# Hybrid streaming layer: x transposed by the host and multiplied strip by strip, two tiles at once, with other stages moved

## The chip, the cores and the metric

One core of a Trainium2 chip runs the whole program; the other cores are idle. The metric is the device time of one execution in microseconds. A core has five engines with a queue each: TensorE (PE, matrix products), VectorE (DVE), ScalarE (ACT), GpSimd (POOL) and SyncE (SP), which issues nearly all DMAs. They run side by side and meet through semaphores. The order of the instructions of each engine is written out by hand in this kernel.

## The reference

One layer for 1024 prompt frames and 32 sample frames together (T = 1056 columns), all in float32:

```python
n = rmsnorm(h, g_mix[l])
z = n @ w_in[l]                       # (1056 x 1024) @ (1024 x 3072)
a_out, s_re, s_im = ssm_branch(u_ssm, ...)      # S5: 32 groups, 64 complex states each
p_out, p_hist = pool_branch(u_pool, ...)        # trailing means of 2, 4, 8, 16 frames
merged = sigmoid(gate_ssm) * a_out + sigmoid(gate_pool) * p_out
h = h + merged @ w_out[l]
n2 = rmsnorm(h, g_ffn[l])
h = h + (silu(n2 @ w_ffn_gate[l]) * (n2 @ w_ffn_up[l])) @ w_ffn_down[l]   # inner width 2816
y = rmsnorm(h, g_final)
```

The factor 1/rms of rmsnorm is a number for each frame, so it commutes with the product: the kernel multiplies x times gain by the weights first and scales the columns of the result behind it. The outputs are y, the last complex states and the last 15 inputs of the pooling branch, for both groups.

## The kernel before

**Precision and slabs.** Each product runs in three passes on split operands: w_hi by x_hi, w_hi by x_lo, w_lo by x_hi. A slab is 128 columns of a weight matrix, 128 x 1024. SyncE loads it into one of two `stage` slots, ScalarE's `split` (line 705) copies it to w_hi, GpSimd's `lo` (line 891) makes w_lo. A tile is 128 output rows by 1056 columns: eight k steps, three passes and three column blocks of 352 give 72 matmuls (`tile`, line 461) into `bank_a` or `bank_b`. It waits until the tile two before has been taken out of its bank (`evac_done`). Slab s may be loaded when `lo_ready` has reached s - 1.

**Head.** SyncE loads x in nine tiles of 128 frames. TensorE turns each one (line 486), VectorE writes it twice, as xg (times g_mix) and as x_raw (line 964), the second for a spill to `xt_scratch`, from which hT is read much later. ScalarE squares the rows (line 721) and makes x_hi, GpSimd makes x_lo. Fifteen small loads bring the parameters, which TensorE turns also (`turn_parameters`). Tile 0 goes by passes (line 514), tiles 1 to 3 follow; these four are the state-space input u. `inverse_root` makes 1/rms on VectorE with a root on ScalarE, `rstd_rows` (line 473) spreads it over all partitions by products of ones with `diag`, `take_rows` copies it to `rstd_row`, and `take_u` (on line 934, where nearly all two-operand operations of VectorE are) scales u into UT.

**State-space parameters.** VectorE computes in a long row of small operations an angle, whose sine ScalarE takes (line 739), then BD, BB, PW, and from these CA (ends at line 1121) and WT. TensorE multiplies BD by CA to K (line 534), turns WT to W (line 545, copied by ScalarE at line 749). GpSimd clears TO when WT is done, then SyncE puts K_sb into TO with sixteen loads (line 348) and fetches U from `u_scratch` with eight (line 354). 128 small products of W and U (line 582) give V, copied into S (line 768). Then VectorE scans S along time in steps spread over the pool groups.

**Pool groups.** Group g is five tiles: the pooled input, two gates and two short tiles of nine matmuls on the pooled values pl_hi and pl_lo. VectorE sums and scales; `gate_t` (line 1277) is scaled by the second product. Both short tiles use bank_b, so the second waits for the scaling of the first. After group 0 stands the V stage. SyncE's order around it: slab 6, u_scratch, slab 7 (pool weights), TO, U, then slabs 8 and 9 for group 1, and CA_st.

**The rest.** Gates, the products of TO with U and CA_st with S_st (lines 603, 604), four transposes of the last states (line 609), the gated units, the output product, the feed-forward part and the final norm. It is not changed but for where hT comes from.

## Time and profile before

| | |
|---|---|
| median of three runs | 1383.84 us (1382.25 to 1385.69) |
| span of the profiled execution | 1384.4 us |
| TensorE, VectorE | busy 1334.2 us, 681.9 us |
| ScalarE, GpSimd | busy 304.8 us, 307.8 us |
| moved by DMA | 95.64 MB, mean 69 GB/s |

All times of the trace are from the start of the span of the profiled execution. Read a line of a timeline as: start, duration, engine, line of the kernel, operation, what it writes and reads; several equal ones in a row are one line with their count, and the bracket tells how long the engine was idle before and what released it. Matmuls overlap, so the duration of one is longer than the distance between two.

### The profile page before, as it was taken

Reading aid. Unit: us, or ns where it says so; the run is one execution under the profiler, and the core shown is the slowest. Engines: PE = TensorE matmul, PEld = TensorE weight load, DVE = VectorE, ACT = ScalarE, POOL = GpSimd, SP = SyncE. Lnnn points to the kernel's source line nnn. Section 1 sums busy time; section 2 is a strip of 40 time slices with the busy share of each in tenths; the row PEclk is TensorE's granted clock in tenths of the full one; section 3 lists DMA queues with packets and bytes.
Section 4 is the critical chain, followed back from the end, with each engine's and each line's share of the span. In section 5 each row is a group of like instructions: output and inputs, shape, how many; then the busy total and the mean of one; then the engine's idle time right before and its main releaser. Section 6 shows DMA issues by size and latency. Waiting matters only on the chain.

```text
span 1384.4 us, 19221 instructions
## 1 busy us (share of the span) xinstructions
PE 1334.2 (96%) x8306; PEld 1320.3 (95%) x8306; DVE 681.9 (49%) x696; ACT 304.8 (22%) x325; POOL 307.8 (22%) x131
## 2 busy tenths in 40 slices
PE   6999699999999999999999999999999999999997
PEld 5988599999999999999999999999999999999996
DVE  5895279860546643324434343434343434343355
ACT  6112221142432222212111111111111111111124
POOL 6111121221222224412222222222222222211210
PEclk9999899999999999999999999999999999999998
DMA  8408641224303351111111111111111111111103
GB/s 258 112 16 145 96 113 66 80 74 101 131 25 92 107 182 40 44 43 46 47 45 45 45 45 45 45 45 43 42 40 42 44 45 45 45 45 46 46 16 126
DMA packets 134895, 95.64 MB, mean 69 GB/s; under 512 B 15165, under 2 KB 122973, under 8 KB 134858
## 3 DMA queue, kind: packets, MB, share of 16 engines
q1 hardware_dynamic: 134794, 95.10, 24.5%
q8 instruction: 26, 0.43, 0.1%
q14 instruction: 11, 0.09, 0.0%
q10 hardware_dynamic: 64, 0.02, 0.0%
HBM read 74.40 MB, written 17.43 MB: 66 GB/s over the span
## 4 chain that ended last, share of the span: by engine, by line
PE 81%; DVE 11%; issue 3%; SPq 2%; DMA 2%; POOL 0%; ACT 0%; DVEq 0%
PE bank_a L461 39%; PE bank_b L461 38%; DMA stage<-in_w_in 1%; DVE f_u L934 1%; DVE hT L934 1%; SPq L348 1%; PE aux L582 1%; DVE tmp_a L934 1%; DVE tmp_b L934 1%; SPq L354 1%; DVE sc_a L934 1%; SPq L322 1%; DVE S L934 1%; DVE pt L934 0%; DVE UT L934 0%
## 5 line engine op out<-in xcount | busy, mean ns | idle before, releaser
L891 POOL TENSOR_TENSOR w_lo<-stage,w_hi 128x1024 fp32r<-128x1024 f32 x110 | 260.8, 2371 | 996.3 <-ACT w_hi L705 996.3
L705 ACT ACTIVATE w_hi<-stage 128x1024 fp32r<-128x1024 f32 x110 | 114.0, 1037 | 797.4 <-PE bank_b L461 495.4
L461 PE MATMUL bank_b<-hg_hi,w_hi 128*128 128x352 f32 x528 | 114.8, 326 | 0.0
L461 PE MATMUL bank_b<-hg_lo,w_hi 128*128 128x352 f32 x528 | 114.7, 325 | 0.0
L461 PE MATMUL bank_a<-hg_lo,w_hi 128*128 128x352 f32 x528 | 114.2, 324 | 0.0
L461 PE MATMUL bank_a<-hg_hi,w_hi 128*128 128x352 f32 x528 | 113.8, 323 | 0.0
L461 PE MATMUL bank_b<-hg_hi,w_lo 128*128 128x352 f32 x528 | 113.8, 324 | 0.0
L461 PE MATMUL bank_a<-hg_hi,w_lo 128*128 128x352 f32 x528 | 113.2, 323 | 0.0
L934 DVE TENSOR_TENSOR hT<-bank_a,hT 128x1056 f32<-128x1056 f32 x48 | 60.2, 1255 | 80.6 <-PE bank_a L461 80.6
L934 DVE TENSOR_TENSOR hT<-bank_b,hT 128x1056 f32<-128x1056 f32 x48 | 60.4, 1258 | 76.2 <-PE bank_b L461 76.2
L934 DVE TENSOR_TENSOR f_u<-bank_b,rstd_row 128x1056 f32<-128x1056 f32 x22 | 27.7, 1257 | 142.6 <-PE bank_b L461 142.6
L461 PEld LDWEIGHTS bank_b<-hg_hi,w_lo 128*128 128x128 f32 x528 | 90.6, 189 | 0.0
L461 PEld LDWEIGHTS bank_b<-hg_hi,w_hi 128*128 128x128 f32 x528 | 90.3, 189 | 0.1
L461 PEld LDWEIGHTS bank_b<-hg_lo,w_hi 128*128 128x128 f32 x528 | 90.3, 188 | 0.0
L461 PEld LDWEIGHTS bank_a<-hg_hi,w_lo 128*128 128x128 f32 x528 | 90.1, 188 | 0.0
L461 PEld LDWEIGHTS bank_a<-hg_lo,w_hi 128*128 128x128 f32 x528 | 89.8, 188 | 0.0
L461 PEld LDWEIGHTS bank_a<-hg_hi,w_hi 128*128 128x128 f32 x528 | 89.8, 188 | 0.0
L461 PE MATMUL bank_a<-x_hi,w_hi 128*128 128x352 f32 x408 | 88.5, 325 | 0.8 <-ACT S L768 0.8
L461 PE MATMUL bank_a<-x_lo,w_hi 128*128 128x352 f32 x408 | 88.2, 324 | 0.0
L461 PE MATMUL bank_a<-x_hi,w_lo 128*128 128x352 f32 x408 | 87.6, 323 | 0.0
L934 DVE TENSOR_TENSOR f_g<-bank_a,rstd_row 128x1056 f32<-128x1056 f32 x22 | 27.7, 1257 | 112.6 <-PE bank_a L461 112.6
L461 PE MATMUL bank_b<-x_hi,w_hi 128*128 128x352 f32 x336 | 72.7, 324 | 0.7 <-ACT W L749 0.7
(262 smaller groups left out, 2355.8 us busy)
## 6 DMA issues: line engine op xcount, KB each, us to landing
stage<-in_w_in SPq DMA_DIRECT2D x24, 512.0 KB, 3.7
stage<-in_w_ffn_gate SPq DMA_DIRECT2D x22, 512.0 KB, 3.7
stage<-in_w_ffn_up SPq DMA_DIRECT2D x22, 512.0 KB, 3.6
stage<-in_w_ffn_down SPq DMA_DIRECT2D x22, 512.0 KB, 3.7
mp_scratch<-gate_t SPq DMA_DIRECT2D x8, 528.0 KB, 3.5
pool_t<-mp_scratch SPq DMA_DIRECT2D x8, 528.0 KB, 3.8
hT<-xt_scratch SPq DMA_DIRECT2D x8, 528.0 KB, 7.5
x_t<-in_x_prompt SPq DMA_DIRECT2D x8, 512.0 KB, 7.0
```

The source lines that it names most:

```text
L322: sp.dma_start(dst, src).then_inc(prm_in, 16)
L348: sp.dma_start(TO[16 * i:16 * i + 16, g2:G:2, 16 * j:P], K_sb[16 * g2:16 * g2 + 16, :, 0:P - 16 * j]).then_inc(to_in, 16)
L354: sp.dma_start(U[16 * i:16 * i + 16, :, :], u_dram[:, L - 1 - i, :].rearrange("(g h) c -> h g c", h=H)).then_inc(u_in, 16)
L461: mm = pe.matmul(banks[:, b, 0:BLK], w[:, slot, col:col + P], x[:, k, b * BLK:(b + 1) * BLK], start=(i == 0 and step == 0), stop=(i == len ...
L582: mm = pe.matmul(aux[64 * g2:64 * g2 + 64, (pr + 1) % 2, comp * NCG:(comp + 1) * NCG], W[:, comp, pr, 64 * g2:64 * g2 + 64], U[:, 2 * pr + ...
L705: act.activation(w_hi[:, slot, 0:cols], stage[:, slot, 0:cols], ACT.Copy).then_inc(hi_ready, 1)
L891: pool.tensor_tensor(w_lo[:, slot, 0:cols], stage[:, slot, 0:cols], w_hi[:, slot, 0:cols], ALU.subtract).then_inc(lo_ready, 1)
L934: return dve.tensor_tensor(out, a, b, op)
```

## The change

- The host passes x transposed and the parameters laid out as the kernel wants them; two outputs leave in a layout that the host puts back.
- TensorE's transposes of x and of parameters, x_raw, xg and the spill go. SyncE loads eight strips of 128 channels by 1056 frames. ScalarE makes x_hi from each with the gain as its scale, VectorE x_lo. TensorE multiplies each strip into tiles 0 and 1 as it comes; the w_lo pass of both follows.
- The rows of x are still loaded and squared, now beside the tiles and through four buffers. The row products stand behind tile 2.
- ScalarE copies u unscaled out of the banks (`raw_u`); VectorE scales the four tiles in SBUF (`scale_u`) once the rows are there, behind PW.
- VectorE takes up pool group 0 (`take_pool`) between CA and WT; TensorE makes K behind tile 5 and W behind tile 6. ScalarE splits slab 8 ahead of taking W, with the root, the sine and the sigmoids in other places.
- SyncE fetches U ahead of TO.
- The short tiles of a pool group use both banks, which change roles from group to group; the loop over groups 1 to 3 on TensorE is unrolled. The pool history leaves by ScalarE's queue from UP, the last states by one copy and one store.

```diff
-            for tt in range(6):
+                if tt >= XT_SLOTS:
+                    sp.wait_ge(x_squared, tt - XT_SLOTS + 1)
+                sp.dma_start(x_t[0:tok(tt), tt % XT_SLOTS, :], src).then_inc(x_in[tt], 16)
+            sp.dma_start(gains[:], t_in["p_gains"]).then_inc(gains_in, 16)
+            load_xs(0)
+            slab(0, 0, [(slab3(0)[:, 0:4], w_in[:, 0:4, 0:P])])
+            slab(1, 1, [(slab3(1)[:, 0:4], w_in[:, 0:4, P:2 * P])])
+            load_xs(1)
+            load_xs(2)
+            for s in range(2):
+                sp.dma_start(slab3(s)[:, 4:8], w_in[:, 4:8, s * P:(s + 1) * P]).then_inc(second_in[s], 16)
+            for k in range(3, KD):
+                load_xs(k)
+            sp.dma_start(prm[:], t_in["p_prm"]).then_inc(prm_in, 16)
+            sp.dma_start(ident[:], t_in["c_ident"]).then_inc(consts_in, 16)
+            for tt in range(XT_SLOTS):
                 load_x(tt)
-            slab(0, 0, [(slab3(0), w_in[:, :, 0:P])])
...
-            spill_x(sp, 0)
-            slab(1, 1, [(slab3(1), w_in[:, :, P:2 * P])])
...
-            sp.dma_start(inv_count[:], t_in["c_inv_count"]).then_inc(inv_in, 16)
-            with nc.allow_non_contiguous_dma(reason="512 skip weights, one per (channel, group)"):
-                for dst, src in prm_loads:
-                    sp.dma_start(dst, src).then_inc(prm_in, 16)
-            for tt in range(4, TT):
-                spill_x(sp, tt)
             for s in (2, 3):
                 slab(s, s % 2, [(slab3(s % 2), w_in[:, :, s * P:(s + 1) * P])])
+            sp.dma_start(b_raw[:], t_in["p_b"]).then_inc(bc_in, 16)
+            sp.dma_start(CT[:], t_in["p_c"]).then_inc(bc_in, 16)
+            sp.dma_start(inv_count[:], t_in["c_inv_count"]).then_inc(inv_in, 16)
+            sp.dma_start(pool_hist[:], t_in["p_hist"]).then_inc(inv_in, 16)
+            sp.dma_start(state0[:], t_in["p_state"]).then_inc(inv_in, 16)
+            sp.dma_start(d_skip[:], t_in["p_skip"]).then_inc(inv_in, 16)
+            for tt in range(XT_SLOTS, TT):
+                load_x(tt)
             slab(4, 0, [(slab3(0), w_in[:, :, W_SSM:W_SSM + P])])
             slab(5, 1, [(slab3(1), w_in[:, :, 2 * W_SSM + D:2 * W_SSM + D + P])])
...
-            sp.wait_ge(evac_done, KS)
+            sp.wait_ge(u_scaled, KS)
             sp.dma_start(u_dram.rearrange("(n p) j c -> p n j c", p=P), UT[:, :, :, :]).then_inc(ut_out, 16)
             pool_w_slab(0)
+            sp.wait_ge(ut_out, 16)
+            for i in range(L):
+                sp.dma_start(U[16 * i:16 * i + 16, :, :],
+                             u_dram[:, L - 1 - i, :].rearrange("(g h) c -> h g c", h=H)).then_inc(u_in, 16)
             sp.wait_ge(k_ready, 1)
             sp.wait_ge(to_zero, 1)
...
+            for k in range(KD):
+                pe.wait_ge(x_hi_ready, k + 1)
+                for n in range(2):
+                    if k == 0:
+                        pe.wait_ge(first_half, n + 1)
+                    if k == KD // 2:
+                        pe.wait_ge(hi_ready, n + 1)
+                    pair_pass(k, n, w_hi, x_hi, k == 0, False)
+                pe.wait_ge(x_lo_ready, k + 1)
+                for n in range(2):
+                    pair_pass(k, n, w_hi, x_lo, False, False)
+            for n in range(2):
+                pe.wait_ge(lo_ready, n + 1)
                 for k in range(KD):
...
+                    mm = pair_pass(k, n, w_lo, x_hi, False, k == KD - 1)
+                mm.then_inc(tile_done, 1)
+            pe.wait_ge(lo_ready, 3)
+            tile(2, bank_a, 0, ALL, x_hi, x_lo)
+            rstd_rows(1, diag)
+            pe.wait_ge(lo_ready, 4)
+            tile(3, bank_b, 1, ALL, x_hi, x_lo)
+            def turn_k():
+                pe.wait_ge(ca_ready, 1)
...
-            def pool_group(g, after_first=None):
+            def pool_group(g):
                 s0, t0 = 4 * g + S_POOL, 5 * g + T_POOL
+                odd, even = (bank_b, bank_a) if g % 2 else (bank_a, bank_b)
                 pe.wait_ge(lo_ready, s0 + 1)
-                tile(t0, bank_a, 0, ALL, x_hi, x_lo)
-                if after_first is not None:
-                    after_first()
+                if g == 0:
+                    pe.wait_ge(row_used, 1)
+                tile(t0, odd, 0, ALL, x_hi, x_lo)
                 pe.wait_ge(lo_ready, s0 + 2)
-                tile(t0 + 1, bank_b, 1, ALL, x_hi, x_lo)
+                tile(t0 + 1, even, 1, ALL, x_hi, x_lo)
+                if g == 0:
+                    turn_k()
                 pe.wait_ge(lo_ready, s0 + 3)
-                tile(t0 + 2, bank_a, 0, ALL, x_hi, x_lo)
+                tile(t0 + 2, odd, 0, ALL, x_hi, x_lo)
+                if g == 0:
+                    turn_w()
                 pe.wait_ge(lo_ready, s0 + 4)
                 pe.wait_ge(pooled_lo, g + 1)
                 hi, lo = pl_hi[:, :].unsqueeze(1), pl_lo[:, :].unsqueeze(1)
-                tile(t0 + 3, bank_b, 1, [(0, 0)], hi, lo)
-                if not isinstance(g, int):
-                    pe.wait_ge(np_evac, g)
-                pe.transpose(aux[0:HIST, 0, 0:P], UP[:, SEQ:SEQ + HIST], ident[:, :])
-                pe.transpose(aux[0:HIST, 0, P:2 * P], UP[:, T + HIST:T + 2 * HIST], ident[:, :]).then_inc(np_turned, 1)
-                pe.wait_ge(evac_done, t0 + 4)
-                tile(t0 + 4, bank_b, 1, [(P, 0)], hi, lo)
-            pool_group(0, turn_w)
+                tile(t0 + 3, even, 1, [(0, 0)], hi, lo)
+                tile(t0 + 4, odd, 1, [(P, 0)], hi, lo)
+            pool_group(0)
...
+            def half(s, h):
+                act.wait_ge((second_in if h else stage_in)[s], 16)
+                cols = slice(h * SLAB // 2, (h + 1) * SLAB // 2)
+                act.activation(w_hi[:, s, cols], stage[:, s, cols], ACT.Copy).then_inc(hi_ready if h else first_half, 1)
+            def take_hi(k):
+                act.wait_ge(xs_in[k], 16)
+                act.activation(x_hi[:, k, :], xs[:, k, :], ACT.Copy, scale=gains[:, 0, k:k + 1]).then_inc(x_hi_ready, 1)
+            def square(tt):
+                act.wait_ge(x_in[tt], 16)
+                row = x_t[0:tok(tt), tt % XT_SLOTS, :]
+                act.activation(row, row, ACT.Square, accum_out=ss[0:tok(tt), 0, tt:tt + 1]).then_inc(x_squared, 1)
+            def raw_u(n):
+                act.wait_ge(tile_done, n + 1)
+                banks = bank_b if n % 2 else bank_a
+                for b0, nb, c0, nch, to in ((0, 2, 0, 44, 0), (2, 1, 88, 40, 88), (2, 1, 128, 4, NCP + 1)):
+                    o = UT[:, n, :, to:to + nb * nch].rearrange("p j (b c) -> p b c j", b=nb)
+                    off = 0 if c0 != 128 else 40 * L
+                    i0 = banks[:, b0:b0 + nb, off:off + nch * L].rearrange("p b (c j) -> p b c j", j=L)
+                    ins = act.activation(o, i0, ACT.Copy)
+                ins.then_inc(evac_done, 1)
+            act.wait_ge(gains_in, 16)
+            take_hi(0)
+            half(0, 0)
+            half(1, 0)
+            take_hi(1)
+            take_hi(2)
+            half(0, 1)
+            half(1, 1)
+            for k in range(3, KD):
+                take_hi(k)
...
+            square(0)
+            square(1)
+            split(2, 0, landed(2), 1)
+            raw_u(0)
+            square(2)
+            split(3, 1, landed(3), 2)
+            raw_u(1)
+            for tt in range(3, TT):
+                square(tt)
...
             root(1)
+            split(4, 0, landed(4), 3)
+            act.wait_ge(row_ready, 1)
+            raw_u(2)
             act.wait_ge(angle_ready, 1)
             act.activation(pt[:, 8:10, :], pt[:, 6:8, :], ACT.Sin).then_inc(sine_ready, 1)
-            for s in range(2, 6):
-                split(s, s % 2, landed(s), s - 1)
-            act.wait_ge(x_lo_ready, TT)
+            split(5, 1, landed(5), 4)
+            raw_u(3)
+            split(6, 0, landed(6), 5)
             for q in range(4):
                 act.wait_ge(k_turn, q + 1)
...
             for g in range(4):
                 s0, t0 = 4 * g + S_POOL, 5 * g + T_POOL
-                split(s0 + 2, 0, landed(s0 + 2), t0 + 1)
+                if g:
+                    split(s0 + 2, 0, landed(s0 + 2), t0 + 1)
                 act.wait_ge(pooled_ready, g + 1)
                 act.activation(pl_hi[:, :], (sum_b if g % 2 == 0 else sum_a)[:, 0:T], ACT.Copy).then_inc(pooled_hi, 1)
-                for r in range(2):
-                    split(s0 + 3 + r, 1 - r, landed(s0 + 3 + r), t0 + 2 + r, cols=(2 * P, SLAB)[r])
-                    act.wait_ge(evac_done, t0 + 2 + r)
-                    act.activation(gate_t[:, r, :], gate_t[:, r, :], ACT.Sigmoid).then_inc(gp_sig, 1)
+                act.dma_start(t_out["pool"][:, 0, g, :], UP[:, SEQ:SEQ + HIST]).then_inc(pool_out, 16)
+                act.dma_start(t_out["pool"][:, 1, g, :], UP[:, T + HIST:T + 2 * HIST]).then_inc(pool_out, 16)
+                split(s0 + 3, 1, landed(s0 + 3), t0 + 2, cols=2 * P)
+                if g == 0:
+                    split(s0 + 4, 0, landed(s0 + 4), t0 + 3)
+                    take_w()
+                    sigmoid_p(0, 0)
+                    sigmoid_p(0, 1)
+                else:
+                    sigmoid_p(g, 0)
+                    split(s0 + 4, 0, landed(s0 + 4), t0 + 3)
+                    sigmoid_p(g, 1)
                 split(s0 + 5, 1, landed(s0 + 5), t0 + 5)
...
-            for s in range(1, 5):
+            for s in range(7):
                 lo(s, s % 2)
             pool.wait_ge(wt_ready, 1)
             pool.memset(TO[:, :, :], 0.0).then_inc(to_zero, 1)
-            for s in range(5, S_GATE):
+            for s in range(7, S_GATE):
                 lo(s, s % 2, 2 * P if s % 4 == 3 else SLAB)
...
+            dve.wait_ge(gains_in, 16)
+            for k in range(KD):
+                dve.wait_ge(xs_in[k], 16)
+                dve.wait_ge(x_hi_ready, k + 1)
+                dve.scalar_tensor_tensor(x_lo[:, k, :], xs[:, k, :], gains[:, 0, k:k + 1], x_hi[:, k, :], MUL,
+                                         SUB).then_inc(x_lo_ready, 1)
...
+            def scale_u(n):
+                dve.wait_ge(evac_done, n + 1)
+                tt_(UT[:, n, :, :], UT[:, n, :, :], rstd_u[:, :, :], MUL).then_inc(u_scaled, 1)
...
-            take_rows(1)
-            take_u(0)
+            dve.wait_ge(x_squared, TT)
+            dve.wait_ge(consts_in, 16)
+            inverse_root(1, ss[:, 0, :], diag)
             dve.wait_ge(sine_ready, 1)
...
-            take_u(1)
+            take_rows(1)
+            dve.tensor_copy(rstd_u[:, :, 0:NCP], rstd_row[:, 0:SEQ].rearrange("p (c j) -> p j c", j=L))
+            dve.memset(rstd_u[:, :, NCP:NCP + 1], 0.0)
+            dve.memset(UT[:, :, :, NCP:NCP + 1], 0.0)
+            then(dve.tensor_copy(rstd_u[:, :, NCP + 1:NCG], rstd_row[:, SEQ:T].rearrange("p (c j) -> p j c", j=L)))
+            for n in range(KS):
+                scale_u(n)
+            dve.wait_ge(u_scaled, KS)
...
-            take_u(2)
+            take_pool(0)
             dve.wait_ge(ca_ready, 1)
...
-                for r, banks in enumerate((B3, A3)):
+                for r in range(2):
                     dve.wait_ge(tile_done, t0 + 2 + r)
                     if g:
                         dve.wait_ge(mp_out[r], 16 * g)
-                    tt_(b3(gate_t[:, r, :]), banks, b3(rstd_row[:, :]), MUL).then_inc(evac_done, 1)
+                    elif r == 0:
+                        dve.wait_ge(to_in, 32 * L)
+                    tt_(b3(gate_t[:, r, :]), bank3(t0 + 1 + r), b3(rstd_row[:, :]), MUL).then_inc(evac_done, 1)
```

## Rows read from the trace of the kernel before

**Rows 1.** The page, busy us, share and number of instructions of each engine.

```profile
PE 1334.2 (96%) x8306; PEld 1320.3 (95%) x8306; DVE 681.9 (49%) x696; ACT 304.8 (22%) x325; POOL 307.8 (22%) x131
```

**Rows 2.** Waits of TensorE in the whole span: us in total, times, longest.

```profile
PE bank_b L461 <- DVE gate_t L1277: 8.0, 4, 2.9
PE aux L582 <- DMA U<-u_scratch: 6.7, 1, 6.7
PE bank_a L486 <- DMA x_t<-in_x_prompt: 4.8, 1, 4.8
```

**Rows 3.** Windows: busy us and count per engine, PEclk, DMA share, GB/s.

```profile
10.00:15.00 5.00, 4.40 (x20) 3.66 (x19) 5.00 (x6) 5.00 (x8) 4.50 (x2) 1.00 1.03 370
...
26.00:30.00 4.00, 3.96 (x14) 3.99 (x15) 0.00 (x0) 2.17 (x2) 4.00 (x3) 0.50 0.80 148
...
205.00:280.00 75.00, 73.65 (x458) 73.31 (x457) 65.11 (x123) 12.44 (x15) 14.64 (x7) 1.00 0.21 71
```

**Rows 4.** Timeline of the head: start, us, engine, line, operation, count, idle before.

```profile
10.32 1.04 ACT L721 ACTIVATE x_sq<-x_t 128x1024 f32<-128x1024 f32 x1
...
26.05 6.55 PE L514 MATMUL bank_a<-x_hi,w_hi 128*128 128x352 f32 x24 [2.39 <-DVE x_raw L964]
...
35.99 1.36 DVE L934 TENSOR_TENSOR diag<-ident,ss 128x1152 f32<-128x1152 f32 x1
...
45.42 1.95 PE L473 MATMUL aux<-diag,ones 128*128 128x128 f32 x16
...
47.63 0.75 PE L461 MATMUL bank_b<-x_hi,w_hi 128*128 128x352 f32 x3
```

**Rows 5.** Timeline of VectorE, 48 to 180 us.

```profile
52.53 0.91 DVE L1062 MEMSET BD<- 128x1024 f32 x1
...
66.36 2.13 DVE L934 TENSOR_TENSOR UT<-bank_b,rstd_row 128x704 f32<-128x704 f32 x3
...
73.39 4.63 DVE L934 TENSOR_TENSOR CA<-tmp_a,tmp_b 128x2304 f32<-128x2304 f32 x1
...
87.50 2.27 DVE L934 TENSOR_TENSOR tmp_a<-BB,PW 128x2048 f32<-128x2048 f32 x1
```

**Rows 6.** Timeline of GpSimd, 37 to 180 us.

```profile
72.39 3.23 POOL L891 TENSOR_TENSOR w_lo<-stage,w_hi 128x1024 fp32r<-128x1024 f32 x1 [9.23 <-ACT w_hi L705]
101.21 3.52 POOL L904 MEMSET TO<- 128x4096 f32 x1 [25.60 <-DVE WT L934]
```

**Rows 7.** Timeline of TensorE, 80 to 180 us.

```profile
85.74 8.84 PE L534 MATMUL aux<-CA,BD 128*32 128x128 f32 x64 [2.96 <-DVE CA L1121]
...
164.11 0.74 PE L461 MATMUL bank_a<-x_hi,w_hi 128*128 128x352 f32 x3 [0.78 <-ACT S L768]
```

**Rows 8.** Timeline of SyncE's DMA queue, 37 to 180 us.

```profile
107.56 12.36 SPq L348 DMA_DIRECT2D TO<-K_sb  x16
```

**Rows 9.** The chain that ended last, 0 to 420 us: start, us, what.

```profile
133.97 15.51 DMA stage<-in_w_in
...
152.79 10.56 PE aux L582 x120
...
284.02 3.00 PE bank_b L461 x9
...
326.19 0.61 PE aux L609 x4
```

**Rows 10.** Timeline of ScalarE, 37 to 180 us.

```profile
94.61 0.59 ACT L745 ACTIVATE K_sb<-aux 32x512 f32<-32x512 f32 x1 [1.16 <-PE aux L534]
...
108.19 1.09 ACT L749 ACTIVATE W<-aux 128x512 f32<-128x512 f32 x2 [0.26 <-PE aux L545]
...
124.47 1.28 ACT L759 ACT_TABLE_LOAD   x1
125.76 1.09 ACT L759 ACTIVATE gate_t<-gate_t 128x1056 f32<-128x1056 f32 x1
```

**Rows 11.** The page, DMA issues: count, KB each, median us from issue to landing.

```profile
stage<-in_w_in SPq DMA_DIRECT2D x24, 512.0 KB, 3.7
```

More of the change, by code:

```diff
@@ L136, in hybrid_layer @@
         ut_at = q_space + G * P + 2 * PAIRS * 9 * H + 2 * PAIRS * P
-        _, diag = overlay(("pad4", [P, ut_at], F32), ("diag", [P, TT, P], F32))
+        w_at = q_space + G * P + 2 * PAIRS * 9 * H
+        _, x_t = overlay(("pad17", [P, w_at], F32), ("x_t", [P, XT_SLOTS, D], F32))
+        _, diag, rstd_u = overlay(("pad4", [P, w_at], F32), ("diag", [P, TT, P], F32), ("rstd_u", [P, L, NCG], F32))
         _, UP, sum_a, sum_b = overlay(("pad5", [P, ut_at], F32), ("UP", [P, T + 2 * HIST], F32),
@@ L507, in _ @@
-            pe.wait_ge(xraw_ready, TT)
-            for w, x, ready, count in ((w_hi, x_hi, x_hi_ready, TT), (w_lo, x_hi, lo_ready, 1), (w_hi, x_lo, x_lo_ready, TT)):
-                pe.wait_ge(ready, count)
-                if w is w_hi:
-                    pe.wait_ge(hi_ready, 1)
-                for k in range(KD):
-                    for b in range(3):
-                        mm = pe.matmul(bank_a[:, b, 0:BLK], w[:, 0, k * P:(k + 1) * P], x[:, k, b * BLK:(b + 1) * BLK],
-                                       start=(w is w_hi and x is x_hi and k == 0), stop=(x is x_lo and k == KD - 1))
-                if w is w_hi and x is x_hi:
-                    turn_parameters()
@@ L518, in _, with pair_pass @@
-            mm.then_inc(tile_done, 1)
-            for s in range(4):
-                if s:
-                    pe.wait_ge(lo_ready, s + 1)
-                    tile(s, bank_b if s % 2 else bank_a, s % 2, ALL, x_hi, x_lo)
-                if s == 0:
-                    pe.wait_ge(prm_used, 2)
-                    rstd_rows(1, diag)
-            pe.wait_ge(ca_ready, 1)
-            pe.wait_ge(row_used, 1)
-            for q in range(4):
-                if q >= 2:
-                    pe.wait_ge(k_evac, q - 1)
-                for i in range(4):
-                    for comp in range(2):
-                        mm = pe.matmul(aux[0:2 * H, q % 2, i * P:(i + 1) * P], BD[:, comp, 4 * q + i, :],
-                                       CA[:, comp, 4 * q + i, 0:P], start=(comp == 0), stop=(comp == 1))
-                mm.then_inc(k_turn, 1)
+            def pair_pass(k, n, w, x, first, last):
+                banks = bank_b if n else bank_a
+                for b in range(3):
+                    mm = pe.matmul(banks[:, b, 0:BLK], w[:, n, k * P:(k + 1) * P], x[:, k, b * BLK:(b + 1) * BLK],
+                                   start=first, stop=last)
+                return mm
@@ L585, in _ @@
             pe.wait_ge(v_evac, PAIRS)
-            with pe.Fori(1, 4) as g:
+            for g in range(1, 4):
                 pool_group(g)
@@ L1085, in bc_h @@
                 return ap.unsqueeze(2).to_broadcast([P, PAIRS, H])
[L1086 to L1087 removed]
+            dve.wait_ge(bc_in, 32)
             t1, t2 = [t[:, 0:PAIRS * H].rearrange("p (q h) -> p q h", h=H) for t in (tmp_a, tmp_b)]
@@ L1138, in _ @@
             tt_(wt[1], mid_of(tmp_a), mid_of(tmp_b), ADD).then_inc(wt_ready, 1)
-            then(dve.memset(UT[:, :, :, NCP:NCP + 1], 0.0))
-            take_u(3)
             dve.wait_ge(k_evac, 4)
+            dve.wait_ge(inv_in, 64)
             lag0 = K_sb[:, :, 0:H]
@@ L1431 @@
     r = run_bass_kernel_spmd(nc, [{f"in_{n}": a for n, a in arrays.items()}], core_ids=[0])
-    return tuple(r.results[0][f"out_{n}"] for n in OUTPUTS)
+    y_p, y_s, state, pool = (r.results[0][f"out_{n}"] for n in OUTPUTS)
+    state = state.reshape(2, NS, 2, 2, PAIRS).transpose(2, 3, 4, 0, 1).reshape(2, 2, 1, 1, G, NS)
+    pool = pool.transpose(1, 3, 2, 0).reshape(2, 1, 1, HIST, W_POOL)
+    return (y_p, y_s, state[0, 0], state[0, 1], pool[0], state[1, 0], state[1, 1], pool[1])
```

311 lines of the change are left out of this document (96 added, 215 removed).

## The prediction

> **What bounds the kernel now.** I read the page first: TensorE is busy for 96% of the span [rows 1]. Each idle stretch of TensorE is therefore time, and almost nothing else is. Its waits [rows 2] add up to little. But a busy TensorE is not always a useful one: until 26 us it only turns x. The first product comes at 26.05 us, its 24 matmuls take 6.55 us, and tile 1 begins only at 47.63 [rows 4], although the DMA engines bring 370 GB/s in the meantime [rows 3]. From there on a tile of 72 matmuls takes 11.6 us. So the head holds about 25 us that a better order could give back. Then I read VectorE from 50 to 113 us: it has no gap. It makes PW, CA and WT one after the other [rows 5]. Behind WT hang the clearing of TO on GpSimd [rows 6], sixteen loads of TO [rows 8], the loads of U and then one weight slab that needs 15.5 us [rows 9]; TensorE waits 3.0 us for CA [rows 7] and 6.7 for U [rows 2]. The question is thus not what the head saves but whether this second chain starts earlier.
>
> I call T the moment at which the first tile of pool group 1 starts (line 461, behind the 128 small products of line 582). Before, T is 164.1 us [rows 7].
>
> **The change, part by part.**
>
> *Head.* The 72 transposes of x, the copies to x_raw and the spills go. The first strip of x is 528 KB behind one small load, like the first x_t behind the identity: it lands at 4.8 us [rows 2]. A table load of 1.28, a scaled copy of 1056 elements 1.1, half a slab 0.6 [rows 10]: TensorE starts at 7.8. Everything up to strip 7 is 5.4 MB, at 370 GB/s [rows 3] in by 16.6 us, and TensorE reaches strip 7 at about 24: the transfers are hidden. Two tiles are 23.3 us, and a cold start costs 6.55 - 3.9 = 2.6 us (granted clock 0.50, the 1.2 GHz level, in 26 to 30) [rows 3, 4]. GpSimd makes w_lo of both slabs while VectorE makes x_lo from two SBUF operands. In the trace such an operation stands still while GpSimd's runs: CA's third takes 4.63 us, not 2.6 (2.27 for 2048 elements), beside w_lo at 72.39, which is itself stretched [rows 5, 6]. Bounds here are 0 and 2.2 us, as TensorE has some reserve; I take 0.8. Tile 1 ends at 7.8 + 23.3 + 2.6 + 0.8 = 34.5 us, against 47.6 + 11.6 = 59.2 before: 25 us.
>
> *From tile 1 to the sine.* ScalarE now does, in its written order, the split of slab 3 (1.06), the raw copy of u (not in the trace: 1056 elements from PSUM, between 1.1 for a contiguous copy [rows 10] and 2.13 for VectorE's strided UT [rows 5]; I take 1.8, nearer the same access), and squares 3 to 8. Loads 6 to 8 wait for squares because of the four buffers, and are there some us before their turn. Six squares at 1.04 + 0.19 are 7.4 us [rows 4]. Then table and root 1.5, VectorE's five small steps and diag 2.4 [rows 4]. The split of slab 4 comes right behind the root, so GpSimd's w_lo meets diag: 2.2 us more by [rows 5, 6], none if they miss each other; I take 2.2. Then row products on TensorE 2.3 [rows 4], raw copy of tile 2 1.8, table and sine 1.5. Sum: 34.5 + 1.06 + 1.8 + 7.4 + 1.5 + 2.4 + 2.2 + 2.3 + 1.8 + 1.5 = 56.5 us. BD and PW come behind it; before, BD began at 52.5 [rows 5]. So the 25 us are gone here: queued squares and row sums stand before the sine. TensorE waits some 5 us for diag.
>
> *From the sine to CA.* BD, BB and PW take 52.53 to 66.3 = 13.8 us with one meeting with GpSimd [rows 5]: 70.3. Taking the rows 1.4 (71.7): only now may tile 4 start, while tile 3 ended near 65. Then rstd_u and its fills 2.0 and four scalings (1.26 contiguous to 2.13 strided [rows 5]; both operands are contiguous, so 1.26) 5.1; they replace four take_u of 2.13. CA takes 68.4 to 85.7 = 17.3 [rows 5, 7]: ready at 96.1. TensorE from 71.7 with two tiles and 2.0 for a cold start (below the 2.6 seen) is at 97.0. It sets the start of the K products, not 85.7 as before.
>
> *From K to WT.* The last K copy ends 9.5 us behind the first product (85.7 to 95.2 [rows 7, 10]) and stands ahead of pl_hi in ScalarE's order; pl_hi and pl_lo take 2.4. VectorE, which now pools group 0 ahead of WT, waits for both: 97.0 + 9.5 + 2.4 = 108.9. WT takes 87.5 to 101.2 = 13.7 us [rows 5, 6]: 122.6.
>
> *From WT to T.* Clearing TO 3.5 [rows 6]; sixteen issues 12.4 [rows 8]; then slab 8, which ScalarE must split before it may take W. U is fetched ahead of TO here, so slab 8 no longer stands behind U and lands 3.7 us after its issue, the median [rows 11]; the other bound is 15.5 [rows 9]. 122.6 + 3.5 + 12.4 + 3.7 = 142.2. The split 1.06, four pairs of W copies at 1.35 = 5.4, two short tiles 3.5 (two sigmoids and a table load beside them, 3.5), split of slab 9 1.06, the 128 small products 10.6 [rows 9] and 0.7 around them. T = 164.5. Against 164.1 it is 0.4 us later: what the wait for U cost before is back as a wait for W behind slab 8.
>
> *Behind T.* The second half of each pool product goes to the other bank now and no longer waits for the scaling of the first: 8.0 us in four groups [rows 2]. The one in group 0 is inside T. In group 1 I count 1.3 us (the gate on VectorE still has to come), in group 2 1.2; in group 3 VectorE is 2.5 us ahead by then, and the half that took 3.0 us on a low clock [rows 9] instead of 1.7 is shorter: 2.3. The four state transposes (0.6 [rows 9]) and the wait ahead of them save 1.0. Sum 5.8. The smaller moves (one state store, laid out parameters, hT read from the input) lie beside products of TensorE that run without a gap after 330 us: nothing. The seven parameter loads ahead of slab 4 cost SyncE some 0.4 us each in a stretch where that slab isn't due for 5 us; their landing is covered likewise.
>
> *Sum.* 1384.4 + 0.4 - 5.8 = 1379.0 in the profiled execution. That one is 0.56 us over the median of the runs, so 1378.4 us.
>
> **Rivals.**
> 1. The head's gain survives. It would need CA by about 85; then tiles 4 and 5 run without pause: 1384.4 - 22 - 2 is about 1360. For it speak the 25 us; against it the written order: sine behind six squares, root and rows. Chance 0.12.
> 2. VectorE holds the pool groups. It is 87% busy from 205 to 280 [rows 3]; if its scan steps set the pace, only 2 of the 5.8 us are kept: 1382. Chance 0.20.
> 3. Slower: slab 8 lands late. If it needs 15.5 us also behind TO's transfers, ScalarE can't take W and T moves by 11.8: 1390. It decides from a landing of 9 us on (13 for clearly slower). For it: this very wait stood at 133.97 [rows 9]; against it: there it stood behind U. Chance 0.12.
> 4. The head doesn't do what it says: the clock stays low through most of two tiles, or strided copies on ScalarE take 2.5 us: 1384. Chance 0.08.
> 5. A table switch costs more than its load. If ScalarE stood for as long again behind the loads for root and sine, both come 2.6 us later: 1381. In the trace a sigmoid follows its load at once (124.47 + 1.28, then 125.76 [rows 10]). Chance 0.04.
>
> The Trainium skill, page "ScalarE: Activation LUTs", section What ACT_TABLE_LOAD costs, counts 1.38 us of drain on top of each load, which as an estimate makes 2.8 us for rival 5; the trace's sigmoid doesn't bear it out.
>
> **How the numbers follow.** The forecast has 0.44. Its own bounds: without the meetings with GpSimd (3.0), with raw copies of 1.1 (1.4) and issues of TO at 0.6 each (2.6) it is 1371; with 2.2 for 0.8, scalings of 2.13 (3.5) and colder W products (1.5) it is 1385. For eight in ten I go to 1368 and 1388, which leaves out most of rivals 1 and 3. About 0.3% (4.2 us) is what a measurement can tell from no change, so faster means below 1379.7. Of the forecast's 0.44, 0.34 lie there; with 0.12 of rival 1, 0.05 of rival 2 and 0.01 of rival 5, faster has 0.52. Slower is above 1388: 0.10 of rival 3 and 0.02 of rival 4, 0.12. The rest is 0.36.
>
> **What would show it.** In the trace after: tile 1 done near 34.5 with no wait for x behind the first; the root after 45 us; TensorE idle before the row products and before tile 4 (some 5 and 7 us); the first K product near 97; a long wait in the W transposes until ScalarE has split slab 8, near 143; T near 164.5; waits on gate_t below 5 us together. I am wrong if the sine comes before 50 us, if T is below 158, or if U is waited for.

## The result, and the profile after

The changed kernel takes 1368.09 us (median of 4 runs, 1366.7 to 1370.48) against 1384.63 for the kernel before in the same measurement (4 runs, 1382.25 to 1385.69): a ratio of 0.9887, 95% interval 0.9873 to 0.9902, or 16.5 us less. I had forecast 6.2 us less, 1378.4, with a range from 1368 to 1388. The direction was right, the size was not: the gain is more than twice what my sum has.

The page of the changed kernel, busy us, share and number of instructions of each engine (before: [rows 1]):

```profile
PE 1303.2 (95%) x8204; PEld 1291.7 (95%) x8204; DVE 672.0 (49%) x672; ACT 312.7 (23%) x334; POOL 292.2 (21%) x122
```

Its waits of TensorE in the whole span, us in total, times, longest (before: [rows 2]):

```profile
PE aux L473 <- ACT W L698: 20.4, 1, 20.4
PE bank_a L428 <- ACT w_hi L634: 8.4, 1, 8.4
PE bank_a L410 <- issue: 7.2, 1, 7.2
PE aux L473 <- DVE WT L887: 4.8, 1, 4.8
PE aux L547 <- DVE sq_sum L887: 3.9, 1, 3.9
PE bank_b L410 <- DVE gate_t L887: 3.6, 2, 2.0
PE aux L422 <- DVE diag L887: 2.5, 1, 2.5
PE bank_a L428 <- DVE x_lo L898: 0.8, 1, 0.8
```

The wait for U is gone and one of 20.4 us for W has come, as forecast. Now TensorE's timeline from 20 to 200 us (start, us, engine, line, operation, count, idle before). Line 410 is the tile's product, 422 the row products, 461 the K products, 473 the W transposes, 507 the small products:

```profile
48.23 3.23 PE L422 MATMUL aux<-diag,ones 128*128 128x128 f32 x16 [2.48 <-DVE diag L887]
...
71.11 1.22 PE L410 MATMUL bank_a<-x_hi,w_hi 128*128 128x352 f32 x3 [7.22 <-issue]
...
120.37 1.84 PE L473 MATMUL aux<-ident,WT 128*128 128x128 f32 x8 [4.78 <-DVE WT L887]
142.66 5.46 PE L473 MATMUL aux<-ident,WT 128*128 128x128 f32 x24 [20.44 <-ACT W L698]
...
162.09 0.75 PE L410 MATMUL bank_b<-x_hi,w_hi 128*128 128x352 f32 x3 [0.49 <-ACT S L727]
```

The last row is T. It was 164.11 [rows 7], I forecast 164.5, and it is 162.09. So of the 18.6 us between the two spans (1384.4 and 1365.8) only 2.0 lie ahead of T. The other 16.6 lie behind it, where my sum has 5.8.

Where are they? No wait there is long enough. But TensorE makes more products in the same time. The windows of both kernels count them (us, busy us of PE and its instructions, PEclk, DMA share, GB/s). The kernel before:

```profile
340.00:440.00 100.00, 99.88 (x619) 1.00 0.29 87
...
1200.00:1300.00 100.00, 99.87 (x620) 1.00 0.16 48
```

The kernel after:

```profile
340.00:440.00 100.00, 99.85 (x625) 1.00 0.28 85
...
1200.00:1300.00 100.00, 99.86 (x624) 1.00 0.14 43
```

Both run the same code there, at the full granted clock (1.00, the 2.4 GHz level), without a gap. Yet 100 us hold 619 or 620 products of 352 columns before and 624 or 625 after: 100 / 619.5 is 161.4 ns each, 100 / 625 is 160.0. Taken from the starts of successive products over the whole trace (some 7,600 distances, those from 150 to 175 ns), the spacing is 161.34 ns before and 160.07 after. A difference of 1.3 ns is invisible in any one row. Over 7,600 products it is 10 us, just what my sum lacks.

### The profile page after: what moved, and what is told of

Read it like the earlier page. It is cut to its first block, busy times and chain, and to the rows that moved or that the text cites. A ratio compares the mean times of both kernels' runs of the same rounds, so it can differ in the third digit from the quotient of the medians.

```text
span 1365.8 us, 18937 instructions
## 1 busy us (share of the span) xinstructions
PE 1303.2 (95%) x8204; PEld 1291.7 (95%) x8204; DVE 672.0 (49%) x672; ACT 312.7 (23%) x334; POOL 292.2 (21%) x122
## 4 chain that ended last, share of the span: by engine, by line
PE 85%; DVE 7%; issue 3%; ACT 2%; DMA 1%; SPq 1%; POOL 1%; DVEq 0%; ACTq 0%
PE bank_b L410 40%; PE bank_a L410 40%; DVE f_u L887 1%; DVE hT L887 1%; SPq L310 1%; DVE sc_a L887 1%; PE aux L507 1%; DVE S L887 1%; DMA xs<-in_x_turned 1%; PE bank_a L428 1%; PE aux L461 1%; DMA stage<-in_w_in 0%; ACT w_hi L623 0%; PE aux L527 0%; DVE sc_b L887 0%
## 5 line engine op out<-in xcount | busy, mean ns | idle before, releaser
L851 POOL TENSOR_TENSOR w_lo<-stage,w_hi 128x1024 fp32r<-128x1024 f32 x110 | 264.5, 2405 | 998.9 <-ACT w_hi L623 987.6
L410 PE MATMUL bank_a<-x_hi,w_hi 128*128 128x352 f32 x360 | 78.4, 327 | 7.2 <-issue 7.2
L410 PE MATMUL bank_b<-x_hi,w_hi 128*128 128x352 f32 x360 | 77.6, 324 | 1.0 <-POOL w_lo L851 0.5
L410 PE MATMUL bank_a<-x_lo,w_hi 128*128 128x352 f32 x360 | 78.0, 325 | 0.0
L410 PE MATMUL bank_a<-x_hi,w_lo 128*128 128x352 f32 x360 | 77.8, 325 | 0.0
```

The costliest lines, as they stand in the source:

```text
L410: mm = pe.matmul(banks[:, b, 0:BLK], w[:, slot, col:col + P], x[:, k, b * BLK:(b + 1) * BLK], start=(i == 0 and step == 0), stop=(i == len ...
L851: pool.tensor_tensor(w_lo[:, slot, 0:cols], stage[:, slot, 0:cols], w_hi[:, slot, 0:cols], ALU.subtract).then_inc(lo_ready, 1)
```

## Experiments: the spacing

The loops from 340 us on are unchanged. What the change does alter for them is where their operands lie. It drops new_pool (4096 bytes per partition) and log_dt (8 bytes, for which 32 are set aside), and shrinks out_state from 2048 to 256. All three stand ahead of the region in which x_hi, x_lo, hg_hi, hg_lo, f_hi and f_lo are laid over each other. So x_hi moves from byte 40512 to 34592. The strips of these tensors are 4224 bytes long and a third of a strip is 1408, both whole multiples of 128, so every moving operand of a kernel has the same remainder by 128 as x_hi: 64 before, 32 after. The weights w_hi and w_lo lie ahead of the dropped tensors, at remainder 0 in both.

Theory: placement sets the spacing. Rival: the code does (the unrolled pool groups, or less traffic by the other engines). Five kernels move the region by an unused tensor and change nothing else, each as this one does, with 8, 16 or 24 columns (32, 64 or 96 bytes):

```
         out_state = sb("out_state", ...)
+        fill = sb("fill", [P, 8])
         zeros = sb("zeros", [P, 16])
```

**before_shift32.** 

> The kernel before with an unused tensor of 32 bytes per partition ahead of zeros; nothing else. The first of the tensors that are laid over each other (x_hi) starts at byte 40544 instead of 40512. Theory 'placement': products are spaced by where their moving operand lies. Remainders of 40512 and of after's 34592 by 128 are 64 and 32; if an odd multiple of 32 makes the 160.0 ns of after, this kernel (remainder 96) shows 160.0 ns between the starts of two products in place of 161.4, and with some 7600 products it gains 10 us: 1374. Rival 'the code' (one edit of the change, unrolled pool groups or less traffic, makes the spacing): spacing stays 161.4 and time stays 1384.6.

Measured: 1389.05 us, ratio 1.0039 (1.0027 to 1.0052); spacing 162.21 ns. Placement matters, but the wrong way: "an odd multiple of 32 is fast" has fallen.

**before_shift64.** 

> The kernel before with an unused tensor of 64 bytes per partition ahead of zeros: x_hi at byte 40576, remainder 0 by 128 and by 64. Placement in its form 'odd multiples of 32 are fast': 161.4 ns as before, 1384.6. Placement in its form 'only a remainder of 64 is slow': 160.0 ns, 1374. Rival 'the code': 161.4 ns, 1384.6.

Measured: 1386.46 us, ratio 1.0018 (1.0008 to 1.0028); spacing 161.72 ns. Slower than the kernel before, so "only a remainder of 64 is slow" has fallen as well.

**after_shift32.** 

> The changed kernel with an unused tensor of 32 bytes per partition ahead of zeros: x_hi at byte 34624, remainder 64 by 128, as in the kernel before. Placement: spacing rises from 160.0 to 161.4 ns and the time from 1368.1 to some 1378, that is what I had forecast. Rival 'the code': 160.0 ns and 1368.

Measured: 1377.09 us, ratio to the kernel before 0.9957 (0.9943 to 0.9971); spacing 161.36 ns. Thirty-two unused bytes cost the changed kernel 9.0 us, and the spacing is that of the kernel before to 0.02 ns.

**after_shift96.** 

> The changed kernel with 96 bytes: x_hi at byte 34688, remainder 0 by 128. 'Odd multiples of 32 are fast': 161.4 ns, 1378. 'Only a remainder of 64 is slow': 160.0 ns, 1368. It must agree with before_shift64 if the remainder decides and not the place itself. Rival 'the code': 160.0 ns, 1368.

Measured: 1378.6 us, ratio 0.9959 (0.9944 to 0.9973); spacing 161.68 ns, that of before_shift64. Both have remainder 0. So two different kernels with the same remainder agree to 0.04 ns, and the rule isn't odd or even: each remainder has its own spacing. Only 32 had not been tried in the kernel before.

**before_shift96.** 

> The kernel before with an unused tensor of 96 bytes ahead of zeros: x_hi at byte 40608, remainder 32 by 128, the one remainder that only the changed kernel has had. Placement (the remainder by 128 sets the spacing: 64 gave 161.35, 0 gave 161.7, 96 gave 162.2 ns, in both kernels alike): 160.0 ns here too, some 10 us less, 1374, without any other edit of the change. Rival (the lower region, or the code together with the remainder): spacing at or above 161.3 and 1384 or more.

Measured: 1376.81 us, ratio 0.9952 (0.9935 to 0.9968); spacing 160.02 ns. Its windows, columns as above:

```profile
340.00:440.00 100.00, 99.83 (x625) 1.00 0.30 92
...
1200.00:1300.00 100.00, 99.85 (x624) 1.00 0.16 47
```

The spacing is what was expected, without any edit of the change. The time fell by 7.0 us in the median, where 10 were expected, and by 9.9 in the profiled span (1374.5), with 10.1 less behind T. The two differ because the profiled execution of the kernel before is a long one: its span is 1384.4 us, those of its seven executions in this measurement are 1380.6 to 1382.6. Of these there is no trace, so where they are shorter stays open.

Next: is it the moving operand's own place, or its distance from the weights? A 32-byte tensor ahead of stage moves both; w_hi and w_lo then have remainder 32.

```
+        fill = sb("fill", [P, 8])
         stage = sb("stage", [P, 2, SLAB])
```

**after_all32.** 

> The changed kernel with an unused tensor of 32 bytes ahead of stage: weights (w_hi, w_lo) and moving operands both move by 32 bytes, weights to remainder 32, x_hi to remainder 64. If the moving operand's own remainder decides: 161.35 ns and 1377, as in after_shift32. If its distance from the weights decides: 160.0 ns and 1368, since that distance is after's. Something between: both have a part.

Measured: 1370.59 us, ratio 0.9894 (0.9869 to 0.992); spacing 160.07 ns although x_hi has remainder 64 now. Two of the four executions took 1367.2 and 1367.3 us, the changed kernel's time, and two 1373.9 and 1374.4. The profiled one is the longest. Its span is 6.5 us over the changed kernel's, 4.1 of them up to T (166.15) and 2.4 behind. In the head VectorE's diag and GpSimd's w_lo meet the other way round:

```profile
48.01 2.34 POOL L852 TENSOR_TENSOR w_lo<-stage,w_hi 128x1024 fp32r<-128x1024 f32 x1 [9.77 <-ACT w_hi L624]
48.08 3.48 DVE L888 TENSOR_TENSOR diag<-ident,ss 128x1152 f32<-128x1152 f32 x1
```

TensorE waited 5.5 us for diag instead of 2.5. Behind T the granted clock fell after a wait of 2.0 us in group 3, where the changed kernel has 1.00 behind the same wait; the products there took some 1.5 us longer (columns as in the windows above):

```profile
284.00:286.00 2.00, 2.00 (x9) 0.54 0.66 270
```

**after_w32** has the tensor ahead of stage and one of 24 columns ahead of zeros as well. 

> The changed kernel with 32 unused bytes ahead of stage and 96 more ahead of zeros: the weights move by 32 (remainder 32 by 128), x_hi by 128 to byte 34720 (remainder 32, as in the changed kernel). Distance decides: it is 0 by 128 here, as in before_shift64 and after_shift96, so 161.7 ns and 1378.5. The moving operand's own remainder decides: 160.0 ns and 1368.

Measured: 1381.31 us, ratio 0.999 (0.9978 to 1.0001); spacing 161.70 ns. The time is 2.8 us over what I expected, and the profiled execution (1379.45) is the shortest of ten, so the trace doesn't tell why. With x_hi at the changed kernel's own remainder its gain is lost, because the weights have moved.

**before_all32** has the tensor ahead of stage alone. 

> The kernel before with 32 unused bytes ahead of stage: weights and x_hi both move by 32, x_hi to remainder 96. Distance decides: it stays 64, 161.35 ns and 1384.3. Own remainder decides: 162.2 ns and 1389, as in before_shift32.

Measured: 1384.08 us, ratio 1.0004 (0.9994 to 1.0013); spacing 161.34 ns. The distance decides, not the operand's own place. All ten kernels in one table:

| distance x_hi from w_hi, remainder by 128 | kernels | spacing, ns |
|---|---|---|
| 32 | after, before_shift96, after_all32 | 160.07, 160.02, 160.07 |
| 64 | before, after_shift32, before_all32 | 161.34, 161.36, 161.34 |
| 0 | before_shift64, after_shift96, after_w32 | 161.72, 161.68, 161.70 |
| 96 | before_shift32 | 162.21 |

The four differ by up to 2.2 ns a product. Times 7,600 that is an estimate of 17 us; the two kernels at the ends, before_shift32 and before_shift96, lie 12.2 us apart in the median and 14.2 behind T in their traces.

Two things the table hides. The price isn't the same for the three passes: in the kernel before, products of w_hi by x_hi, w_hi by x_lo and w_lo by x_hi are on average 161.6, 162.2 and 160.2 ns apart, in the changed kernel 160.1 in each. At distance 0 they are 162.2, 161.4 and 161.5, at 96 they are 161.6, 163.0 and 162.1. Kernels of one distance agree in this pattern to 0.1 ns. And the period of 128 bytes is shown for the remainder 32 alone, where the distances of two kernels differ by 47 times 128. In the rows of 64 and of 0 they differ by 23 times 256 or not at all, so there a period of 256 would fit as well. The distance 96 has one kernel, and no step below 32 bytes was tried.

Why is open. The weights of the next product are loaded while the operand of this one streams (PEld is busy for 95% of the span beside PE's 96% [rows 1]), and a meeting of the two reads would fit. No row shows such a meeting.

With after_shift32 the change can now be taken apart at equal spacing. Its T is 161.73 and its span 1374.9: 2.4 us gained up to T and 7.1 behind it (1220.3 us from T to the end before, 1213.2 now), against -0.4 and 5.8 in my sum. The remaining 9.5 behind T (1213.2 to 1203.7 in the changed kernel) are spacing.

## Experiments: the chain up to T

My forecast says that T hangs on one chain: sine, CA, K, WT, TO, slab 8, W. The next kernels cut it at different links. All are the changed kernel with the edits shown.

**w_first** lets ScalarE take W ahead of slab 8:

```
                 if g == 0:
-                    split(s0 + 4, 0, landed(s0 + 4), t0 + 3)
                     take_w()
+                    split(s0 + 4, 0, landed(s0 + 4), t0 + 3)
```

> The changed kernel with one edit on ScalarE: in group 0 the copies of W stand ahead of the split of slab 8. Theory (the chain WT, TO, slab 8, split, W sets T): TensorE's wait of 20.4 us for W goes, what is late next is VectorE, which can't empty tiles 5 and 6 until the loads of TO have landed (139.97) and so holds tiles 7 and 8 to 141.3. The small products still wait for ScalarE behind the sigmoids and the table load. T goes from 162.1 to some 156.5: 1362.5. Rival (TO's loads hold everything anyway through the copies of S): T stays at 160 or later, 1366 to 1368.

Measured: 1362.5 us, ratio to the kernel before 0.9843 (0.9826 to 0.9859). TensorE's timeline:

```profile
120.28 6.22 PE L473 MATMUL aux<-ident,WT 128*128 128x128 f32 x32 [4.78 <-DVE WT L887]
141.28 1.22 PE L410 MATMUL bank_b<-pl_hi,w_hi 128*128 128x352 f32 x3 [14.78 <-DVE gate_t L887]
...
157.00 0.75 PE L410 MATMUL bank_b<-x_hi,w_hi 128*128 128x352 f32 x3 [0.49 <-ACT S L727]
```

The 20.4 us for W are gone and 14.8 for gate_t stand in their place: VectorE doesn't empty tiles 5 and 6, since gate_t lies over K_sb, from which TO is still being loaded. Only the second half of gate_t does: it has bytes 213024 to 221472, and K_sb begins at 219168. The kernel makes the first half wait too, which no run here undoes. Taking a wait away uncovered the next one, 5.6 us shorter. T is 157.00, forecast 156.5.

**v_first** goes around both:

```
                 if g == 0:
                     turn_w()
+                    turn_v()      # the 128 small products, moved up
                 pe.wait_ge(lo_ready, s0 + 4)
...
-                    split(s0 + 4, 0, landed(s0 + 4), t0 + 3)
                     take_w()
+                    for pr in range(PAIRS): ...   # the copies of S, moved up
+                    split(s0 + 4, 0, landed(s0 + 4), t0 + 3)
...
+            slab(S_POOL + 4, 0, ...)              # SyncE, ahead of TO's loads
             sp.wait_ge(k_ready, 1)
```

> The changed kernel; in group 0 the W transposes and the 128 small products with their copies of S run directly behind tile 6, ahead of the two pool products and the split of slab 8, and slab 8 is fetched ahead of the sixteen loads of TO. Theory: small products 128 to 139, pool products at 141.3 when VectorE has emptied tiles 5 and 6, one sigmoid and its product before bank_b is free: T near 145, 17 us earlier, 1351. Rival (the gain comes back behind T as waits for VectorE, which is busy with the scan): T near 145 but the end only 5 to 10 us earlier, 1358 to 1363.

Measured: 1354.01 us, ratio 0.9792 (0.9775 to 0.9808). The tile of T starts at 144.69, 17.4 us earlier. From there to the end the profiled execution takes 1205.1 us against 1203.7, so nearly all of it stays there. It is the shortest of four (1351.67); in the medians the gain is 14.1 us, 3 less than I expected. The edit moves the small products, the copies of S and the fetch of slab 8 together and doesn't tell their shares apart.

**sine_first** tests the step of the forecast by which the head's 25 us are gone at the sine:

```
             raw_u(1)
+            act.wait_ge(angle_ready, 1)
+            act.activation(pt[:, 8:10, :], pt[:, 6:8, :], ACT.Sin)...
             for tt in range(3, TT):
                 square(tt)
-            root(1)
             split(4, 0, landed(4), 3)
-            act.wait_ge(row_ready, 1)
             raw_u(2)
-            act.wait_ge(angle_ready, 1)
-            act.activation(pt[:, 8:10, :], pt[:, 6:8, :], ACT.Sin)...
+            root(1)
```

VectorE makes BD to PW ahead of the root's steps, and the row products stand behind tile 3. 

> The changed kernel with the sine ahead of squares 3 to 8; VectorE makes BD, BB and PW ahead of the root's steps, the row products stand behind tile 3. This undoes the step of my prediction by which the head's 25 us are gone at the sine. Theory: sine near 38.6, PW done near 52.5, rows taken near 61 instead of 71, tile 4 starts at 61, CA ready near 84.6 instead of 94.6, first K product 12 us earlier, T near 150, 1356. Rival (the order of squares and sine costs nothing, the chain is held by something else, such as the loads of b and c or tile 3): CA not before 92 and 1365 or more.

Measured: 1356.57 us, ratio 0.9803 (0.9787 to 0.982). From its timeline:

```profile
38.39 0.23 ACT L676 ACTIVATE pt<-pt 128x32 f32<-128x32 f32 x1
...
60.55 0.73 PE L410 MATMUL bank_a<-x_hi,w_hi 128*128 128x352 f32 x3 [1.46 <-issue]
84.06 7.17 PE L462 MATMUL aux<-CA,BD 128*32 128x128 f32 x64 [0.20 <-DVE CA L1076]
...
149.37 0.76 PE L410 MATMUL bank_b<-x_hi,w_hi 128*128 128x352 f32 x3 [0.49 <-ACT S L727]
```

Sine at 38.4, tile 4 at 60.6 instead of 71.1, K products at 84.1 instead of 96.7, T 12.7 us earlier. The edit reorders, apart from one wait that it adds on TensorE and two temporaries that it puts elsewhere. So the head's gain had indeed been spent in the queue ahead of the sine.

**both_first** joins the two. 

> The changed kernel with the edits of sine_first and v_first together. Theory (two links of one chain, the first 11.5 us, the second 14): the gains add up, T near 136, 1342.5. Rival (they overlap, because once the chain is short TensorE's own work up to T or VectorE's scan sets the end): 1348 to 1352.

Measured: 1343.96 us, ratio 0.9705 (0.9689 to 0.9721), T at 134.80. The gains nearly add: 24.1 us over the changed kernel, where the two alone gave 14.1 and 11.5, and T 27.3 us earlier, where they gave 17.4 and 12.7. Against the kernel before it is 40.5 us less. What it leaves behind T is a wait in group 1:

```profile
174.91 1.14 PE L412 MATMUL bank_b<-pl_hi,w_hi 128*128 128x352 f32 x3 [3.94 <-DVE gate_t L891]
```

**both_later_scan** goes after it: scan_steps(5, 10) becomes scan_steps(5, 8), and scan_steps(10, 15) becomes scan_steps(8, 15). 

> both_first with two of the five scan steps that VectorE makes between emptying tiles 10 and 11 of group 1 moved behind that group. Theory (these steps, 2.4 us each, hold tile 11's bank): the wait of 3.9 us goes, 1340. Rival (VectorE is then late by as much in group 2): the wait turns up there, 1344.

Measured: 1347.96 us, ratio 0.9743 (0.9726 to 0.9759): 4.0 slower than both_first. Its waits of TensorE:

```profile
PE bank_b L412 <- DVE gate_t L891: 6.5, 2, 4.5
PE bank_a L412 <- DVE gate_t L891: 4.8, 1, 4.8
```

The wait in group 1 is gone and 4.8 us stand in group 2 (at 213.66): in kind the rival. But the rival has 1344, no loss, and the 4.0 us are more than the 0.9 by which the new wait is longer. From T (133.85) to the end the profiled execution takes 1211.0 us against 1208.4; the rest isn't traced. VectorE is what TensorE waits for in these groups, and shifting its work shifted the wait.

**u_last** undoes one move of the change:

```
             pool_w_slab(0)
-            (U fetched here)
             sp.wait_ge(k_ready, 1)
             ... the loads of TO ...
+            sp.wait_ge(to_in, 32 * L)
+            (U fetched here)
```

> The changed kernel with U fetched behind the landing of TO's loads again, so slab 8 is issued behind both. Theory (W, and with it T, hangs on slab 8): TO lands at 140, sixteen loads of U are issued until about 150, slab 8 lands 4 to 6.5 us later, W is taken near 157 and T comes near 178: 1384. If slab 8 needs 15.5 us behind U as it did in the kernel before: T near 187, 1393. Rival (the place of U's loads is indifferent, since U isn't needed before 152): 1368.

Measured: 1389.94 us, ratio 1.0045 (1.0028 to 1.0062). SyncE's queue, then ScalarE:

```profile
122.35 10.56 SPq L305 DMA_DIRECT2D TO<-K_sb  x16
138.10 9.39 SPq L310 DMA_DIRECT2D U<-u_scratch  x8
147.54 8.12 SPq L249 DMA_DIRECT2D stage<-in_w_in  x2
```

```profile
161.95 1.06 ACT L624 ACTIVATE w_hi<-stage 128x1024 fp32r<-128x1024 f32 x1 [57.82 <-DMA stage<-in_w_in]
```

Slab 8 is issued at 147.5 and taken at 162.0, 14.4 us later. In the changed kernel it is issued at 134.60 and taken at 141.06, 6.5 us. So the 15.5 us of [rows 9] belong to the place behind U, not to the slab. T is 182.44, between my two expectations, and the wait for W is 42.9 us. Fetching U early is worth 21.9 us in this order. That it is worth so much because the change puts W behind slab 8 follows from the chain, but isn't shown: no run fetches U late with W ahead of slab 8.

**one_bank** undoes the two banks of the short pool tiles:

```
-                tile(t0 + 4, odd, 1, [(P, 0)], hi, lo)
+                pe.wait_ge(evac_done, t0 + 4)
+                tile(t0 + 4, even, 1, [(P, 0)], hi, lo)
```

The banks also no longer change roles from group to group, as in the kernel before. 

> The changed kernel with both halves of each pool product in the same bank again, the second behind the scaling of the first. My forecast's step (4.8 us for this edit behind T, and what group 0 costs ahead of it): waits of 1.7 to 3 us in front of the second half of each group, 1373 to 1374. Rival (VectorE sets the pace of the groups, so the edit gave only 2 us): 1370.

Measured: 1374.82 us, ratio 0.9939 (0.9923 to 0.9956). The waits of TensorE on gate_t:

```profile
PE bank_b L410 <- DVE gate_t L1209: 9.5, 4, 3.3
```

They are 9.5 us in four groups instead of 3.6 in two. The span is 6.3 us longer, 4.5 of them behind T (1208.2 from there to the end against 1203.7) and 1.8 ahead of it. Of the 4.5 some 1.5 are products at a low granted clock (0.50 from 284 to 286 us, behind the wait in group 3). The kernel before has this stretch as well (0.51), but so has after_all32 with both banks in use, so this part can't be put down to the edit with certainty. Longer waits on gate_t make up most of the rest: behind T they are 7.5 us instead of 3.6, while one of 0.6 us for w_lo goes.

## Why the forecast was wrong, point by point

**The head: right.** Forecast, then measured: tile 1 done 34.5, tile 2 starts 33.95; root done 46.3 by my sum, 45.7; sine done 56.5, 55.7; tile 4 at 71.7, 71.11 with 7.2 us of idle time ahead of it; CA 96.1, 94.6. Three terms were off in both directions. Raw copies of u take 2.13 to 2.18 us, not 1.8: the strided price of VectorE [rows 5] was the nearer row. VectorE's diag was not stretched: it came at 46.82, GpSimd's w_lo began at 46.98 and was the one that stood (3.40 us). TensorE waited 2.5 us for diag, where I had some 5. In after_all32 it is the other way: w_lo began 0.07 us ahead of diag, kept its 2.34 us, and diag took 3.48. In both traces the one that came second stood. I had taken the worse case, and after_all32 has it.

**From K to W: right, 2 us too long.** K's products took 7.2 us instead of 8.8, TO's issues 10.6 instead of 12.4. Slab 8 needed 6.5 us, not 3.7. WT was ready at 120.3 (forecast 122.6), slab 8 landed at 141.1 (142.2), T came at 162.09 (164.5). w_first, v_first and sine_first each moved T to within 1 us of what the chain says, so the mechanism is shown and not only fitted. A row of the kernel before that stands in neither [rows 2] nor my working belongs here:

```profile
PE aux L582 <- ACT new_pool L762: 4.7, 1, 4.7
```

Its small products stood 6.7 us for U and right behind that 4.7 for ScalarE, which could split slab 8 only at 149.50. So slab 8 already came later than U before the change. Rival 1, that the head's gain survives, was wrong for this kernel; sine_first shows an order in which half of it does.

**The pool groups: right in size.** The waits on gate_t fell from 8.0 to 3.6 us (I had below 5). I priced the edit at 4.8 us behind T, 1.3 of them for products at a low clock, and one_bank gives 4.5, some 1.5 of them for the clock. All edits behind T together are 7.1 at equal spacing, not 5.8; the 1.3 between them I haven't traced to a part. Rival 2 fell with it.

**The step that failed: "The smaller moves ... lie beside products of TensorE that run without a gap after 330 us: nothing."** That these stretches have no gap says that nothing waits there. It doesn't say that their products keep their price. Dropping new_pool and log_dt and shrinking out_state moved the operands by 5920 bytes, so that the distance from the weights went from 64 to 32 by 128. That was worth 9.5 us behind T, more than all that I had costed there. With the spacing of the kernel before, the changed kernel takes 1377.09 us, 1.3 from my 1378.4. Part of that closeness is luck: between the two traces the gain at equal spacing is 9.5 us (2.4 up to T, 7.1 behind), where my sum has 5.4. The medians show 7.1 only, as the profiled execution of the kernel before, at 1384.4, is longer than any of its 19 in that measurement (spans 1380.0 to 1383.9). And my range reached to 1368 by widening the bounds of my own terms (1371 to 1385), none of which is the price of a product, so it is luck as well that the time lies at its edge. None of the signs by which I would have known myself wrong came (sine 55.7, T 162.09, no wait for U): all three look ahead of T, and the miss lies behind it.

## What to carry to other kernels

Where one kind of instruction fills nine tenths of the span, a layout edit can change its price: compare the number of products per 100 us in a gapless stretch before looking for waits. Ask of each dropped or shrunk tensor what lies behind it, and try some distances between weights and moving operands on purpose; of the four tried here, 32 bytes apart, one was clearly the best. And when a wait goes, name the next one with its time: w_first gained 5.6 us of a wait of 20.4, and both_later_scan moved a wait from one group to the next.

## What the runs showed of the hardware

The spacing of products of 352 columns (fp32r, back to back, granted clock 1.00) is 160.0, 161.3, 161.7 or 162.2 ns, by the distance between moving operand and weights modulo 128 bytes (32, 64, 0, 96). Within each distance that several kernels have they agree to 0.05 ns, across two different programs. That the period is 128 and not 256 is shown for 32 alone, and 96 rests on one kernel.

The Trainium skill, page "TensorE: Matmul & The Clock Gate", section Back-to-back issue gap, gives N / 2.4 + 2.5 ns for the isolated gap, as an estimate 149.2 ns here, with no term for where operands lie. That is for a single product and not for a stream of weight loads and products like this one; the traces have 160.0 at best, and the measurement decides. The Trainium skill's page "SBUF — State Buffer", section SBUF: two separate sides, says that TensorE has its own port and waits on no other engine. These runs don't speak against it, since the other engines' work is the same in before_shift32, before_shift64, before_shift96 and the kernel before, which have all four spacings; but it doesn't cover what TensorE's own two reads do to each other.

A weight slab of 512 KB was there 6.5 us after its issue behind TO's sixteen loads (the changed kernel), and 14.4 us (u_last) and 15.5 us (the kernel before) behind U's eight. The place in the queue, not the size, set its price.

Of VectorE's diag and GpSimd's w_lo, started within 0.2 us of each other, the one that came second was the one stretched: w_lo to 3.40 us in the changed kernel, diag to 3.48 in after_all32.
